# Softmax steps of a latent attention placed between the tiles of the projection that follows

## What is computed

```python
z = x @ w_in
c_q, c_kv, k_rope, sb_qkv, conv_in, fox_qkv, fox_f, gate_logits = _split_cols(z)
y_a = _mla(c_q, c_kv, k_rope, positions, mla_q_norm, mla_kv_norm, mla_w_uq, mla_w_ukv)
y_b = _stick_breaking(*_split_heads(sb_qkv))
y_c = _conformer_conv(conv_in, conv_w, conv_b, conv_ln_g, conv_ln_b)
y_d = _forgetting_attention(*_split_heads(fox_qkv), fox_f, b_forget)
# _mla, per block of 128 queries and 4 heads:
logits = (q_nope @ k_nope.T + q_rope @ k_rope.T) * scale, masked to key <= query
p = softmax(logits);  out = p @ v
```

## Time and profile before

| what | us |
|---|---|
| median of 3 runs (lowest, highest) | 2858.95 (2851.86, 2873.66) |
| the profiled execution's own time | 2862.46 |
| its span | 2860.7 |
| softmax steps of the latent attention, layer 1 and 2 | 34.4, 34.7 |
| second projection, layer 1 and 2 | 93.9, 93.8 |
| stick-breaking stage, layer 1 and 2 | 48.1, 46.5 |

### The profile page before, as it was taken

One profiled execution on the slowest core, in us unless ns is written; L12 is line 12 of the kernel. 1 busy time (PEld: TensorE's weight loads), 2 busy tenths in 40 slices (PEclk: granted clock), 3 DMA queues, 4 the chain that ended last, 5 costly groups with the idle time before them and its releaser, 6 DMA issues.

```text
span 2860.7 us, 31363 instructions
## 1 busy us (share of the span) xinstructions
PE 2560.1 (89%) x11284; PEld 1843.7 (64%) x11284; DVE 1583.7 (55%) x2277; ACT 1274.7 (45%) x1880; POOL 250.4 (9%) x201
## 2 busy tenths in 40 slices
PE   6899887799999889899996999978989999699996
PEld 2577664477777567577774666635757777466664
DVE  6635476322223357544456788845754445577775
ACT  5423434422222443433324777725354323377773
POOL 0000000000000010000001333201000000032330
PEclk9899998999999899999997999989999999799998
DMA  9411100222113212031224999951202212299994
GB/s 344 160 59 60 34 1 1 88 89 88 59 60 106 90 55 93 1 118 59 89 84 145 333 329 331 332 185 59 89 30 89 88 59 91 94 327 326 340 334 163
DMA packets 197745, 392.18 MB, mean 137 GB/s; under 512 B 23663, under 2 KB 54399, under 8 KB 197631
## 3 DMA queue, kind: packets, MB, share of 16 engines
q1 hardware_dynamic: 170912, 340.55, 33.9%
q10 hardware_dynamic: 14367, 33.34, 3.1%
q0 software_dynamic: 12352, 16.81, 1.8%
HBM read 386.44 MB, written 29.36 MB: 145 GB/s over the span
## 4 chain that ended last, share of the span: by engine, by line
PE 69%; DMA 10%; DVE 9%; ACT 5%; issue 4%; DVEq 2%; SPq 1%; ACTq 0%; POOL 0%; POOLq 0%; PEldq 0%; PEld 0%
PE banks L192 18%; PE banks L193 17%; PE banks L194 17%; PE banks L168 9%; DMA ring<-in_w_exp_up 8%; ACT hT_parts L2954 2%; DMA ring<-in_w_mod 1%; PE banks L1888 1%; PE banks L1896 1%; DVE hT_parts L3057 1%; PE banks L1913 1%; DVE ring_parts L470 1%; DVE ring_parts L3060 1%; SPq L240 1%; PE banks L2197 1%
## 5 line engine op out<-in xcount | busy, mean ns | idle before, releaser
L193 PE MATMUL banks<-ring_parts,arena_parts 128*80 128x512 f32 (+2 forms) x1296 | 514.8, 397 | 0.0
L194 PE MATMUL banks<-arena_parts,ring_parts 128*128 128x512 f32 (+1 forms) x1168 | 456.6, 391 | 0.0
L192 PE MATMUL banks<-arena_parts,hT_parts 128*128 128x512 f32 x1056 | 421.8, 399 | 28.4 <-issue 10.5
L222 DVE TENSOR_TENSOR ring_parts<-ring,hT_parts 128x1024 fp32r<-128x1024 f32 x148 | 181.3, 1225 | 360.0 <-ACT hT_parts L218 356.3
L192 PE MATMUL banks<-hT_parts,arena_parts 128*80 128x512 f32 (+1 forms) x824 | 335.9, 408 | 36.7 <-DVE hT_parts L3057 21.8
L3060 DVE TENSOR_TENSOR ring_parts<-ring,hT_parts 128x2048 fp32r<-128x2048 f32 x128 | 292.7, 2288 | 124.4 <-ACT hT_parts L2954 124.0
L218 ACT ACTIVATE hT_parts<-ring 128x1024 fp32r<-128x1024 f32 x148 | 156.6, 1058 | 442.8 <-PE banks L194 442.0
L193 PE MATMUL banks<-hT_parts 128*128 128x512 f32 x864 | 343.1, 397 | 0.0
L2954 ACT ACTIVATE hT_parts<-ring 128x2048 fp32r<-128x2048 f32 x128 | 244.4, 1911 | 170.3 <-DMA ring<-in_w_exp_up 121.2
L192 PE MATMUL banks<-arena_parts 128*128 128x512 f32 (+3 forms) x712 | 279.5, 393 | 8.2 <-DVEq L161 3.8
L193 PEld LDWEIGHTS banks<-ring_parts,arena_parts 128*80 128x80 f32 (+1 forms) x1296 | 216.4, 167 | 75.7 <-issue 2.6
(11 more groups left out here) (497 smaller groups left out, 3925.2 us busy)
## 6 DMA issues: line engine op xcount, KB each, us to landing
ring<-in_w_exp_gate SPq DMA_DIRECT2D x64, 1024.0 KB, 5.4
ring<-in_w_exp_up SPq DMA_DIRECT2D x64, 1024.0 KB, 8.2
ring<-in_w_exp_down SPq DMA_DIRECT2D x128, 512.0 KB, 6.9
ring<-in_w_in SPq DMA_DIRECT2D x58, 1024.0 KB, 7.2
ring<-in_w_mod SPq DMA_DIRECT2D x24, 1024.0 KB, 13.5
ring<-in_w_gate SPq DMA_DIRECT2D x11, 1024.0 KB, 5.4
ring<-in_w_up SPq DMA_DIRECT2D x11, 1024.0 KB, 8.0
ring<-in_w_down SPq DMA_DIRECT2D x22, 512.0 KB, 4.4
```

The lines of the kernel that those rows point to most:

```text
L192: nc.tensor.matmul(out, lh, rh, start=start and i == 0, stop=False)
L193: nc.tensor.matmul(out, lh, rl, start=False, stop=False)
L194: last = nc.tensor.matmul(out, ll, rh, start=False, stop=stop and i == len(terms) - 1)
L222: nc.vector.tensor_tensor(unit_of(ring_r, n, q), unit_of(ring, n, q), hi_unit(s[1]).bitcast(F32), ALU.subtract).then_inc(S("unit_lo"), 1)
```

## The change

`soft_*` is no longer called for the latent attention, and the rendezvous behind it is gone. The same 16 units are cut into 19 steps (`mla_step_pe`, `mla_step_act`, `mla_step_dve`), and step u stands behind tile 4u // 3 of the second projection: three steps in four tiles, the last behind tile 24. The first 32 tiles (`SHARED`), two of the four jobs, use banks 0 to 3 one after the other, so that the second job waits for the first one's copies; banks 4 and 5 hold the scores, bank 6 the turned pieces, bank 7 the values: one bank and one `mla_pt` buffer where there were two. All eight input parts and the first weight unit are made in stage 1, the unit ahead of the last turned queries and keys. The two Sigmoid copies stand at tile 14, among the exponentials. POOL clears its arrays once the last values are made. Of the 31 taps 7 stand beside the shared tiles, 20 behind the splits of the last two jobs, and 4 in the stick-breaking stage, two behind each of its steps 0 and 1; the layer norm's parts move one step later there.

```diff
-        mla_p = A(19600, 2, LAT)
-        mla_pt = [A(20624, LT, LAT), A(22672, LT, LAT)]
...
+        mla_junk = A(5120, 2, LAT)
+        mla_p = A(6144, 2, LAT)
+        mla_pt = A(7168, LT, LAT)
...
+            parts_hi(act, "px", px_hi[0:4], hT_lat[0:4])
             z0_root(0)
+            parts_hi(act, "px", px_hi[4:6], hT_lat[4:6])
             z0_root(1)
+            parts_hi(act, "px", px_hi[6:], hT_lat[6:])
...
+            pj_first_act(act, R)
...
+            parts_lo(dve, "px", px_hi[0:4], hT_lat[0:4], px_lo[0:4])
             z0_scaled(0)
...
             k_turned(2)
+            pj_first_dve(dve)
             k_turned(3)
...
+        PJ_BANK = (0, 0, 4, 0)
+        SHARED = 8 * LT
+        SCORE_BANK, TURN_BANK, VALUE_BANK = 4, 6, 7
+
+        def soft_at(tile):
+
+            return [u for u in range(UNITS + 3) if 4 * u // 3 == tile]
+
+        def mla_step_pe(pe, u):
+            def scores(u):
+                h, i = divmod(u, LT)
+                w = (i + 1) * P
+                if u >= 2:
+                    pe.wait_ge(S("mla_exp"), u - 1)
...
+
+            def turned(n):
+                if n:
+                    pe.wait_ge(S("mla_ptc"), n)
+                pe.wait_ge(S("mla_pn"), n + 1)
...
+
+            def values(h):
+                pe.wait_ge(S("mla_ptc"), LT * (h + 1))
+                if h == 2:
+                    pe.wait_ge(S("mla_y"), 1)
...
+
+            if u == 0:
+                scores(0)
+            if u + 1 < UNITS:
+                scores(u + 1)
+            if LT < u < UNITS and u % LT == 1:
+                values(u // LT - 1)
+            if 1 <= u <= UNITS:
+                turned(u - 1)
+            if u == UNITS + 2:
+                values(H2 - 1)
+
+        def mla_step_act(act, u):
+            if u < UNITS:
+                w, c = (u % LT + 1) * P, u % 2
+                act.wait_ge(S("mla_max"), u + 1)
+                if u >= 2:
+                    act.wait_ge(S("mla_tr"), u - 1)
+                nc.scalar.activation(mla_p[:, c, 0:w], ps[:, SCORE_BANK + c, 0:w], ACT.Exp, scale=MD ** -0.5, bias=stat[:, c:c + 1],
+                                     accum_out=stat[:, 2 + c:3 + c]).then_inc(S("mla_exp"), 1)
+            if 2 <= u < UNITS + 2:
+                h, i = divmod(u - 2, LT)
+                act.wait_ge(S("mla_tr"), u - 1)
+                if h:
+                    act.wait_ge(S("mla_pv"), h)
+                nc.scalar.activation(mla_pt[:, 0:i + 1, tok_of(i)], ps[:, TURN_BANK, 0:(i + 1) * P].rearrange("p (a b) -> p a b", b=P),
+                                     ACT.Copy).then_inc(S("mla_ptc"), 1)
+            if u in (2 * LT + 2, UNITS + 2):
+                r = u // UNITS
+                act.wait_ge(S("mla_pv"), 2 * r + 2)
+                nc.scalar.activation(yT[:, 0, r, :], ps[:, VALUE_BANK, :], ACT.Copy).then_inc(S("mla_y"), 1)
+
+        def mla_step_dve(dve, u):
+            V = nc.vector
+            c = u % 2
+            if u < UNITS:
+                dve.wait_ge(S("mla_acc"), u + 1)
...
+            if 1 <= u <= UNITS:
+                w, c = ((u - 1) % LT + 1) * P, 1 - c
+                dve.wait_ge(S("mla_exp"), u)
...
 
...
-                        if q == 0 and c >= 2:
-                            pe.wait_ge(S("pj_free"), 4 * (c - 2) + m + 1)
+                        if q == 0 and c % 2:
+                            pe.wait_ge(S("pj_free"), 4 * (c // 2) + m + 1)
+                        if q == 0 and c == 2:
+                            pe.wait_ge(S("mla_y"), 2)
...
-                        last = mm3(ps[:, 4 * (c % 2) + m, :], terms, q == 0, q == 3)
+                        last = mm3(ps[:, PJ_BANK[c] + m, :], terms, q == 0, q == 3)
                         if q == 3:
                             last.then_inc(S("pj_acc"), 1)
-                    if q < 3:
-                        last.then_inc(S("unit_used"), 1)
+                        elif m == 3:
+                            last.then_inc(S("unit_used"), 1)
+                        tile = 4 * LT * c + LT * q + m
+                        for u in soft_at(tile) if tile < SHARED else ():
+                            mla_step_pe(pe, u)
...
+            for tile in range(SHARED):
+                if tile % LT == 0:
+                    split(*divmod(tile // LT + 1, 4))
+                for u in soft_at(tile):
+                    mla_step_act(act, u)
+                if tile == 14:
+                    for j in range(2):
+                        act.wait_ge(S("pj_acc"), j + 1)
+                        A_(c_sig[:, j, :], ps[:, j, :], ACT.Sigmoid)
+                        done()
+                if tile == 16:
+                    for j in range(2):
+                        act.wait_ge(S("pj_acc"), j + 3)
+                        A_(hp[:, j, CW - 1:], ps[:, 2 + j, :], ACT.Copy)
+                        done()
+                    act.drain().then_inc(S("cv_in"), 1)
+                if tile == 25:
+                    forget_act(act)
+            act.wait_ge(S("pj_zero"), 1)
+            qk_tiles(1, s_q, s_k)
...
-                conv_taps(dve, tap_at(n), tap_at(n + 1))
+                n = len(TAP_TILES) + 3 * (4 * c + q - 9)
+                conv_taps(dve, n, min(n + 3, CW - TAPS_SB))
 
             nc.vector.tensor_scalar(sb_mask, u_lt[:, :], -NEG, NEG, ALU.mult, ALU.add)
-            unit_run(0, 3, split)
-            dve.wait_ge(S("pj_zero"), 1)
-            dve.wait_ge(S("cv_in"), 1)
-            nc.vector.tensor_tensor(hp[:, :, CW - 1:], hp[:, :, CW - 1:], c_sig, ALU.mult)
-            dve.drain()
-            for c in range(1, 4):
+            for tile in range(SHARED):
+                if tile % LT == 0:
+                    split(*divmod(tile // LT + 1, 4))
+                for u in soft_at(tile):
+                    mla_step_dve(dve, u)
+                if tile == 17:
+                    dve.wait_ge(S("cv_pad"), 1)
+                    dve.wait_ge(S("cv_in"), 1)
+                    nc.vector.tensor_tensor(hp[:, :, CW - 1:], hp[:, :, CW - 1:], c_sig, ALU.mult)
+                    dve.drain()
+                if tile in TAP_TILES:
+                    n = TAP_TILES.index(tile)
+                    conv_taps(dve, n, n + 1)
+                if tile == 26:
+                    forget_dve(dve)
+            for c in (2, 3):
                 unit_run(c, 3, split_and_tap)
 
+        TAP_TILES = (19, 21, 23, 25, 27, 29, 31)
+        TAPS_SB = 4
 
...
+            nc.gpsimd.memset(hp[:, :, 0:CW - 1], 0.0).then_inc(S("cv_pad"), 1)
+            nc.gpsimd.tensor_copy(f_pick[0:F_ROWS, :, :], ident[0:F_ROWS, 0:H2, None].to_broadcast([F_ROWS, H2, P]))
+            pool.wait_ge(S("mla_pv"), H2)
             for m in (s_q, s_v, f_q, f_v):
                 nc.gpsimd.memset(m, 0.0)
-            nc.gpsimd.memset(hp[:, :, 0:CW - 1], 0.0)
-            nc.gpsimd.tensor_copy(f_pick[0:F_ROWS, :, :], ident[0:F_ROWS, 0:H2, None].to_broadcast([F_ROWS, H2, P]))
...
-                if s == 1:
+                if s == 2:
                     conv_mean_pe(pe)
-                if s == 2:
+                if s == 3:
                     conv_var_pe(pe)
             values(SB_STEPS - 1)
...
-                if s == 3:
+                if s == 4:
                     conv_root_act(act)
...
+                if s < 2:
+                    conv_taps(dve, CW - TAPS_SB + 2 * s, CW - TAPS_SB + 2 * s + 2)
                 if s == 1:
                     fsum_dve(dve)
-                if s == 2:
+                if s == 3:
                     conv_centre_dve(dve)
-                if s == 4:
+                if s == 5:
                     conv_hat_dve(dve)
 
...
                     rendezvous(pe, "pe")
-                    soft_pe(pe, "mla", lambda h, i: mq_t[0:MD, h, tok_of(i)], lambda h, w: mk_t[0:MD, h, 0:w], v_mla, mla_p, mla_pt)
-                    rendezvous(pe, "pe")
                     pj_pe(pe, R)
```

More of the change, by code:

```diff
@@ L1728, in mla_pe, with mla_act @@
             qk_turned(3)
-        def mla_act(act, lay):
+        def mla_act(act, lay, R):
             A_ = nc.scalar.activation
@@ L1983, in build @@
         pj_jobs = ((N_CV, (2, 3, 0, 1)), (N_SB, (0, 1, 2, 3)), (N_VV, None), (N_FX, (0, 1, 2, 3)))
+        PJ_BANK = (0, 0, 4, 0)
[9 more added lines that the diff above has]
+                    pe.wait_ge(S("mla_exp"), u - 1)
+                out = ps[:, SCORE_BANK + u % 2, :]
+                nc.tensor.matmul(out[:, 0:w], mq_t[0:MD, h, tok_of(i)], mk_t[0:MD, h, 0:w], start=True, stop=False)
+                nc.tensor.matmul(out[:, w - P:w], ident_r[:, :], causal_r[:, :], start=False, stop=True).then_inc(S("mla_acc"), 1)
+            def turned(n):
+                if n:
+                    pe.wait_ge(S("mla_ptc"), n)
+                pe.wait_ge(S("mla_pn"), n + 1)
+                for j in range(n % LT + 1):
+                    last = nc.tensor.transpose(ps[:, TURN_BANK, j * P:(j + 1) * P], mla_p[:, n % 2, j * P:(j + 1) * P], ident[:, :])
+                last.then_inc(S("mla_tr"), 1)
+            def values(h):
```

(47 more changed lines are left out.)

45 lines of the change are left out of this document (16 added, 29 removed).

## The result

The median after is 2887.9 us (11 runs, 2878.22 to 2892.65), against 2861.44 us for the kernel before on the same chip (11 runs). The ratio is 1.0081, 95% interval 1.0068 to 1.0094: 0.8% slower. That is within the 1% of the forecast "no change", but 30 us above the predicted 2858 and above the range's upper end of 2874. The profiled execution after took 2878.22 us in all, the lowest of its 11, with a mean granted clock of 0.957; the longest, 2892.65 us, had 0.952. The kernel before had 0.954 in its profile.

A forecast was written before the change was run, and what follows sets the result against it. PE, busy 89% of the span, was taken as the bound. Layer 1: -34.4 + 24.2 + 3.0 + 1.0 + 5.6 = -0.6 us; layer 2 -0.9; together -1.5, against the median 2857.5, predicted 2858 us, range 2843 to 2874.

The forecast's parts named there:

- Waits inside the shared part: 3.0 us: Projection tiles shared with softmax steps: PE waits 3.0 us a layer, mainly turned pieces waiting for ACT's copy; bounds 0, 9.
- The removed stage, -34.4: Softmax steps as their own stage: removing it saves 34.4 us a layer, with its rendezvous and 3.44 us wait.
- PE's work, +24.2: Second projection: PE's work of the 16 softmax units moves in and adds 24.2 us a layer; upper bound 27.0.
- The slow clock, 2.8 us a layer kept: Projection: one slow stretch costing 2.8 us stays within its 93.9 us, expected at the new entry.
- The end of stage 1, +1.0: End of stage 1: first weight split ahead of the last turned queries and keys costs 1.0 us; bounds 0 and 2.3.
- The stick-breaking stage, +5.6: Stick-breaking stage: two taps behind each of steps 0 and 1 make PE wait, +5.6 us; bounds 0 and 7.1.
- The one place of 1.9 us: Between exponentials of steps 11 and 12: table loads, Sigmoid copies and a split take ACT 4.8 us; PE lacks 1.9.
- Rival C: Shared part: the single bank for turned pieces sets the pace, +16 us for both layers, 2874; chance 0.15.
- A: Projection: no slow stretch at entry and shared waits of 1 us win 9.6 us more, 2848; chance 0.17.
- B: Stick-breaking stage: the taps are hidden in PE's idle time, 11 us less, 2847; chance 0.10.
- D: ACT in the shared part: a 1.4 us drain behind each new table load, 5.5 us more, 2863.5; chance 0.04.
- E: Shared part: late projection weights or POOL clears put the steps in series with the projection, 2865; chance 0.07.

The follow-up runs named there:

- the second profile: The changed kernel measured once more, unaltered, for another profile: 2884.04 us (3 runs), ratio to the kernel before 1.0071.
- the first experiment: Changed kernel with the weight splits of tiles 4 to 28 behind the softmax step on ACT and DVE: 2862.13 us, ratio to before 0.9999.
- alone: Kernel before with only its last four taps moved into the stick-breaking stage and the norm's parts one step later: 2874.61 us, ratio 1.0039.
- both: Changed kernel with splits behind the softmax step, four taps back in the projection and norm parts back in place: 2851.6 us, ratio to before 0.9947.
- the placed kernel: Changed kernel with taps back in the projection, forget gate's DVE part at tile 31, splits placed one by one: 2850.9 us, ratio to before 0.9956.

## Why the prediction was wrong

**The step that failed** is "Waits inside the shared part: 3.0 us", of the sum. Measured: 11.4 us of waits for ACT's copies in layer 1. I counted a split as work in its queue (1.06 us on ACT in the thick place). I missed that a split there begins with a wait: from tile 4 on, its buffer comes free only at the end of the tile just before it, so it drags the softmax step behind it to that moment. The earlier trace rows had shown it: before its 15 splits ACT sat idle for 49.0 us, 48.7 of them for L194. PE's idle time of 12.6 us is above the 9 us from which I called myself wrong. That bound had the same gap, since the pace at which the steps ran alone had no split among them. Moving the splits, and nothing else, took 9.4 us of these waits away, and moving them on DVE alone 8.4.

**The removed stage, -34.4, and PE's work, +24.2**, hold. With the splits behind, pj is 120.6 us; these terms and 3.0 of waits make 121.1. That the two totals are so close is in part luck: the waits there are 5.1 us, not 3.0, and the 2.8 us of slow clock inside the 93.9 are gone. 120.6 less 91.1 and 5.1 leaves 24.4 us for PE's work.

**The slow clock, 2.8 us a layer kept.** None came at the new entry, where it was expected; it came behind waits of PE. Behind the third of them in layer 1 the clock fell, and eight value matmuls took 4.03 us for the 2.32 of the earlier trace rows:

```profile
1042.65 4.03 PE L2018 MATMUL banks<-arena 128*128 128x512 f32 x8 [2.04 <-ACT arena L2046]
```

```profile
1040.00:1042.50 2.50, 0.62 (x3) 0.19 (x1) 2.27 (x7) 0.95 (x3) 0.00 (x0) 1.00 0.00 0
1042.50:1047.00 4.50, 4.35 (x11) 2.62 (x12) 0.57 (x3) 0.21 (x2) 0.00 (x0) 0.62 0.00 0
```

PE was busy for 0.62 of 2.5 us, then had a clock of 0.62 over 4.5 us, 1.7 us lost. Layer 2 had that stretch and a longer one that began in its wait of 2.93 us:

```profile
2025.50:2032.50 7.00, 5.93 (x18) 4.87 (x19) 3.73 (x7) 2.10 (x5) 0.00 (x0) 0.51 0.00 1
```

That is 7.0 x 0.49 = 3.4 us lost, where pj is 2.4 us longer than in layer 1. Neither layer 1 nor the second profile has it, with the same waits: a long wait is not always followed by it. In the first experiment the clock over the shared part was 1.00, as the view rounds it, for 0.98 here. So a wait can cost more than its length: 9.4 us less of waits for copies shortened layer 1's projection by 8.7, although the wait at tile 32 grew from 0.7 to 2.8.

**The end of stage 1, +1.0**: measured +0.8 and +0.9 (45.01 for 44.18, 45.13 for 44.26).

**The stick-breaking stage, +5.6**: +5.6 and +6.3 in after, +6.0 and +7.6 alone. The spread is clock: the stage had 0.96 in layer 1 and 1.00 in layer 2 before, worth the 1.6 us between 48.1 and 46.5. At 1.00 on both sides it is 52.4 (first experiment) for 46.5 ("both"), 5.9 us for taps of 5.8. The mechanism is in the trace as it was told: four taps behind the sum of step 0, then the first combination (L2366).

```profile
1140.95 0.42 DVE L2380 TENSOR_TENSOR arena<-arena,banks 128x256 f32<-128x256 f32 x1 [1.38 <-PE banks L2294]
1141.29 2.90 DVE L2196 SCALAR_TENSOR_TENSOR arena<-arena,cols 128x512 f32<-128x512 f32 x4
1144.27 0.69 DVE L2366 SCALAR_TENSOR_TENSOR arena<-banks,arena 128x512 f32<-128x512 f32 x1
```

```profile
1145.02 1.22 PE L2294 MATMUL banks<-arena,n_gt 128*128 128x256 f32 x2 [2.71 <-DVE arena L2366]
```

**The one place of 1.9 us.** A wait behind the table loads is there with the foreseen size, 1.92 us at 1057.54, but it was not the largest (2.94 at 1070.88), and with the splits behind it shrank to 0.48 while both loads stayed. It was the split again, with the loads.

**Rival C**, slower, named the right wait and nearly the right sum (16 us), but not the cause. It did name the splits among its reasons, as work between the chain's steps. Its single bank is still there in every experiment, and the waits for copies went to 2.0 us. No run gave the turned pieces a second bank. What one could have won with the splits ahead can be estimated from the trace: PE would still need the product of the unit (L2066), which stands behind the split as well. It ended at 1019.15, where the copy ended at 1019.67, and 0.2 to 0.5 us before the copy in the other three waits of L2010, 1.7 us of 11.4 in all. The waits above 1 us in after were five (2.65, 1.68, 2.04, 1.92, 2.94), each at a step behind a split, not eleven. A: the clock won 1.1 us in layer 1 and lost in layer 2 while the waits stayed; its slow stretch went in the first experiment, once the waits were short. B: the taps were not hidden. D: no drain shows behind the loads, and both loads together held 0.7 us. E: PE's waits for the chain, not late weights or clears.

**What stays open.** The profiles of the two kernels differ by 15.8 us, the medians by 26.5. The first experiment gained 23 us by the ratios and 17.4 by the spans. The slower executions of after had a lower mean clock (down to 0.951) and more waits give it more places to fall, but no slower execution was profiled, so that is argued, not shown.

## What to carry to other kernels

Before work is put between the steps of a latency chain, ask of each neighbour not only how long it takes but what it waits for first; an instruction that is gated by the slowest engine goes behind the chain's next step in the queue, not ahead of it, unless its wait is over by then: the placed kernel kept the split at tile 18 ahead of the step, three tiles after its buffer came free; ACT started it with no idle time before it, and PE's longest wait for a copy in layer 1 was 0.5 us. The same order counts for an engine that looks idle: DVE was busy for 46% of the shared part, and the order in its queue still held PE up for eight microseconds a layer. Work that is moved out of a stage with room into one without can cost its full length, as the four taps did.

## What was unexpected

Small DVE instructions with one input array were held by POOL's clears. The same 16-column add of the forget gate (L1871) took 2.91 us beside the clears and 0.17 us when the gate came later. First the experiment with both edits, POOL and then DVE:

```profile
1069.63 7.06 POOL L2209 MEMSET arena<- 128x2048 f32 x4 [61.53 <-PE banks L2018]
```

```profile
1071.18 1.23 DVE L222 TENSOR_TENSOR ring_parts<-ring,hT_parts 128x1024 fp32r<-128x1024 f32 x1 [5.89 <-ACT hT_parts L218]
1072.33 1.41 DVE L2201 SCALAR_TENSOR_TENSOR arena<-arena,cols 128x512 f32<-128x512 f32 x2
1073.81 2.91 DVE L1871 TENSOR_SCALAR stat<-f_tmp 128x16 f32<-128x16 f32 x1
```

Then the one with the gate at tile 31:

```profile
1079.13 0.17 DVE L1871 TENSOR_SCALAR stat<-f_tmp 128x16 f32<-128x16 f32 x1
```

The held instruction ended at 1076.72, and the four clears at 1076.69. The instruction right behind it (L1872, two inputs, 2.83 us) ended with it, so its length says nothing about itself. In after the same add took 0.9 us and the next one (L1874) 1.7, and they ended at 1083.22 and 1085.00, within 0.03 us of the ends of the second and the third clear; the reciprocal behind them (L1877) ran beside the fourth at its usual 0.25. The kernel before has it too: L2076 (128 columns, one input) took 3.60 us from 1041.42 and ended at 1045.02, with four clears of 7.12 us in all from 1041.39, so within 0.1 us of where the second ends by their mean length (1.78 us). The split and the taps, with two arrays as inputs, ran beside the same clears at their usual 1.23 and 0.7 us. "SBUF — State Buffer", SBUF: two separate sides, in the Trainium skill tells of a port pair that DVE and GpSimd lock for a whole instruction; DVE needs it in its 2-port modes, and for two-input instructions only against GpSimd work that reads SBUF. The clears here have no input. The rows agree on the lock, since the held instructions ended with a clear, and on the two-input instructions; which mode an instruction ran in no run shows. Moving the gate away won nothing as a whole, since DVE's tail then was the end; but work of this kind beside a clear can't be costed by its length.
